# Six of w_o's eight column chunks as Strassen products, the sums of h in another order, other PSUM banks for FFN chunk 2

## The reference

```
h   = RMSNorm(x)
z   = h @ w_in                       # split among four branches a, b, c, d
y_b = branch_b(z) @ its output weight   # gated MLP, windowed attention, trailing means, conformer conv
merged = sum over the branches of sigmoid(h @ w_gate[b] + b_gate[b]) * y_b
x   = x + RMSNorm(merged @ w_o)
h2  = RMSNorm(x)
x   = x + RMSNorm((silu(h2 @ w_gate_ffn) * (h2 @ w_up_ffn)) @ w_ffn_out)
```

## Time and profile before

| | |
|---|---|
| median of 3 runs | 2610.16 us (2606.91 to 2612.08) |
| the profiled execution | 2609.34 us, of it span 2607.6 us |
| mean granted TensorE clock | 0.991 |
| PE busy | 97% |
| DVE busy | 68% |
| ACT busy | 41% |
| POOL busy | 5% |

### The profile page before, as it was taken

How to read it: one execution, slowest core, us unless ns; L and a number is a source line. 1 busy time by engine, 2 the same in 40 slices (tenths; PEclk the granted TensorE clock), 3 DMA queues, 4 the chain that set the end, 5 groups by cost and what they waited for, 6 DMA issues and landing times.

```text
span 2607.6 us, 41323 instructions
## 1 busy us (share of the span) xinstructions
PE 2536.9 (97%) x17348; PEld 1711.9 (66%) x17348; DVE 1775.5 (68%) x1962; ACT 1070.3 (41%) x1311; POOL 118.0 (5%) x96
## 2 busy tenths in 40 slices
PE   7999998999999999999979999999999999999998
PEld 3444443788788778744437888888888874444443
DVE  7985656787778777722587999999999962222223
ACT  5225432444444444433454455545455442222221
POOL 0000011000000000011320000000000000000002
PEclk9999999999999999999999999999999999999999
DMA  5231122233333233343142333333333343333331
GB/s 212 99 127 65 65 81 75 91 120 109 109 123 113 95 116 115 130 168 100 65 147 85 124 111 114 113 113 114 111 126 103 126 167 103 102 99 102 104 97 64
DMA packets 77737, 287.03 MB, mean 110 GB/s; under 512 B 8624, under 2 KB 9776, under 8 KB 76080
## 3 DMA queue, kind: packets, MB, share of 16 engines
q1 hardware_dynamic: 77616, 285.39, 32.4%
HBM read 276.97 MB, written 8.39 MB: 109 GB/s over the span
## 4 chain that ended last, share of the span: by engine, by line
PE 86%; DVE 7%; issue 3%; ACT 2%; POOL 0%; DMA 0%; DVEq 0%; SPq 0%; ACTq 0%; POOLq 0%
PE psum L1346 15%; PE psum L1347 15%; PE psum L1348 15%; PE psum L1339 13%; PE psum L1340 13%; PE psum L1341 13%; DVE wq L808 1%; ACT wq L460 1%; PE psum L1418 1%; PE psum L1443 1%; DVE region_f L1192 0%; DVE region_t L869 0%; DVE region_f L1180 0%; DVE region_f L1089 0%; DVE std L901 0%
## 5 line engine op out<-in xcount | busy, mean ns | idle before, releaser
L808 DVE SCALAR_TENSOR_TENSOR wq<-stage,wq 128x1024 f16<-128x1024 f32 (+2 forms) x668 | 801.7, 1201 | 687.3 <-ACT wq L460 681.9
L460 ACT ACTIVATE wq<-stage 128x1024 f16<-128x1024 f32 (+2 forms) x668 | 691.0, 1036 | 922.4 <-PE psum L1341 512.7
L1339 PE MATMUL psum<-region_f,wq 128*128 128x512 f16 x1616 | 615.4, 381 | 30.0 <-DVE work L1214 9.5
L1340 PE MATMUL psum<-region_f,wq 128*128 128x512 f16 x1616 | 615.1, 381 | 0.0
L1341 PE MATMUL psum<-region_f,wq 128*128 128x512 f16 x1616 | 615.0, 381 | 0.0
L1348 PE MATMUL psum<-region_t,wq 128*128 128x256 f16 x2176 | 593.6, 273 | 0.0
L1346 PE MATMUL psum<-region_t,wq 128*128 128x256 f16 x2176 | 593.5, 273 | 0.0
L1347 PE MATMUL psum<-region_t,wq 128*128 128x256 f16 x2176 | 593.5, 273 | 0.0
L1346 PE MATMUL psum<-region_f,wq 128*128 128x256 f16 x1632 | 446.3, 273 | 14.8 <-DVE region_t L869 8.9
L1347 PE MATMUL psum<-region_f,wq 128*128 128x256 f16 x1632 | 446.3, 273 | 0.0
L1348 PE MATMUL psum<-region_f,wq 128*128 128x256 f16 x1632 | 446.3, 273 | 0.0
(11 more groups left out here) (189 smaller groups left out, 1925.5 us busy)
## 6 DMA issues: line engine op xcount, KB each, us to landing
stage<-w_ffn_in_chunks SPq DMA_DIRECT2D x176, 512.0 KB, 3.9
stage<-w_gate_chunks SPq DMA_DIRECT2D x128, 512.0 KB, 4.0
stage<-w_ffn_out_chunks SPq DMA_DIRECT2D x64, 448.0 KB, 3.4
stage<-w_in_chunks SPq DMA_DIRECT2D x52, 512.0 KB, 5.3
stage<-w_o_chunks SPq DMA_DIRECT2D x32, 512.0 KB, 3.6
stage<-w_ffn_out_chunks SPq DMA_DIRECT2D x32, 512.0 KB, 3.5
stage<-w_branch_chunks SPq DMA_DIRECT2D x24, 512.0 KB, 3.5
region_f<-x_t SPq DMA_DIRECT2D x4, 1024.0 KB, 9.1
```

The source lines that it names most:

```text
L460: nc.scalar.activation(dst, stage[:, q % STAGES, 0:UNIT_W[u]], ACT.Copy, scale=WSCALE).then_inc(hi_ready, 1)
L808: V.scalar_tensor_tensor(out=slot[:, 1, 0:w], in0=stage[:, q % STAGES, 0:w], scalar=WSCALE, in1=slot[:, 0, 0:w], op0=ALU.mult, op1=ALU.sub ...
L1339: mm(to, w[:, 0, w_at:w_at + P], x_hi, start=start, stop=False)
L1340: mm(to, w[:, 0, w_at:w_at + P], x_lo, start=False, stop=False)
```

## The change

- **h's sums.** The first gates 0, 1 and 2 make three, three and two sums, gate 3 none. Windows 0 and 1 of branch c are finished at `tasks(27)` in place of `tasks(31)`.
- **w_o.** Chunks 0 and 1 stay plain, chunks 2 to 7 become Strassen products. For them merged gets its eight sums in `tset`, through a buffer `t_m` of two: sums 0 and 1 in the last gate, the others under chunks 0 and 1. TensorE waits for all eight low halves ahead of chunk 2. A tile of the output now comes out of `cb`: ACT squares it into one buffer `o_square` and copies it to `mix`. POOL signals each of its adds.
- **FFN.** Chunk 2 goes to banks 4 and 5, chunk 3 to 0 and 1 as before, so chunk 3 waits for chunk 0's eviction alone (`f_gate` 1), and the Strassen stage waits for chunk 2's (`evicted1`).
- The host puts the quarters of w_o's chunks 2 to 7 in the Strassen order. Unit numbers and semaphore targets move along.

The diff, without renumbering of targets and definitions of views:

```diff
@@ -35,6 +35,7 @@
 FFN_TURNS = 10
+FFN_BANK = (0, 2, 4, 0)
 WSCALE = 256.0
@@ -60,7 +61,7 @@
 BRANCHES = (3, 1, 0, 2)
-PLAIN_FFN = 4
+PLAIN_O, PLAIN_FFN = 2, 4
 X_SIZES = (8, 8, 7, 7, 7, 7)
@@ -240,6 +249,7 @@
         cb = view(work, 3 * HS, 2 * S, F32, "p (t s) -> p t s", t=2)
+        o_square = view(work, 3 * HS + 2 * S, S, F32)
@@ -422,11 +432,9 @@
                         pool.wait_ge(osq_ready, 2 * PAIRS * phase + 2 * p + t + 1)
-                        if t == 1:
-                            pool.wait_ge(pool_step, step.up())
-                        ins = nc.gpsimd.tensor_tensor(std[:, :], std[:, :], squares[:, t, :], ALU.add)
-                        ins.then_inc(pool_step if t == 0 else osq_used, 1)
-                    pool.wait_ge(osq_used, PAIRS * phase + p + 1)
+                        src = o_square if phase == 0 and p >= PLAIN_O else squares[:, t, :]
+                        nc.gpsimd.tensor_tensor(std[:, :], std[:, :], src, ALU.add).then_inc(osq_used, 1)
+                        pool.wait_ge(osq_used, 2 * PAIRS * phase + 2 * p + t + 1)
@@ -600,7 +608,8 @@
                 hi(u + 4)
-                t_high(2 * j)
+                if j < 3:
+                    t_high(3 * j)
                 if j == 1:
@@ -610,7 +619,10 @@
                 hi(u + 6)
-                t_high(2 * j + 1)
+                if j < 3:
+                    t_high(3 * j + 1)
+                if j < 2:
+                    t_high(3 * j + 2)
                 evict1(u + 3, sig1_0, ACT.Sigmoid, bias=vecs[:, col + 1:col + 2])
@@ -656,6 +668,11 @@
                     gate(jj, j)
+            def t_high_merged(i):
+                act.wait_ge(t_made, KP + i + 1)
+                nc.scalar.activation(tset[:, :, i, 0, :], t_m[:, i % 2, :, :], ACT.Copy).then_inc(t_hi, 1)
+
+            t_high_merged(0)
             merged_high(PAIRS - 1)
@@ -663,25 +680,65 @@
                 if t == 0 and sums > 0:
-                    act.wait_ge(osq_used, sums)
+                    act.wait_ge(osq_used, 2 * sums)
                 nc.scalar.activation(squares[:, t, :], psum[:, t, :], ACT.Square, scale=UNSCALE).then_inc(osq_ready, 1)
...
             load_sqrt_table()
-            for c in range(PAIRS):
+            t_high_merged(1)
+            t_high_merged(2)
+            for c in range(PLAIN_O):
                 u = U_O + 4 * c
                 hi(u + 4)
+                if c == 0:
+                    t_high_merged(3)
+                else:
+                    t_high_merged(7)
                 hi(u + 5)
                 norm_tile(u + 1, mix, V_POST, 2 * c, c)
+                if c == 0:
+                    t_high_merged(4)
                 hi(u + 6)
-                if c + 1 < PAIRS:
-                    hi(u + 7)
+                if c == 0:
+                    t_high_merged(5)
+                hi(u + 7)
                 norm_tile(u + 3, mix, V_POST, 2 * c + 1, c)
-            hi(U_F + 3)
+                if c == 0:
+                    t_high_merged(6)
+
+            def mixed(c, cs, t):
+
+                j = 2 * c + t
+                act.wait_ge(c_read, 4 * cs + (2 if t else 4))
+                act.wait_ge(osq_used, 2 * c + 1 - t)
+                nc.scalar.activation(o_square, cb[:, t, :], ACT.Square, scale=UNSCALE).then_inc(osq_ready, 1)
+                nc.scalar.activation(mix[:, j, :], cb[:, t, :], ACT.Copy,
+                                     scale=vecs[:, V_POST + j:V_POST + j + 1]).then_inc(evicted1 if t else evicted0, 1)
+
+            def o_chunk(c):
+                u, cs = U_OS + SU * (c - PLAIN_O), CS_O + c - PLAIN_O
+                if c == PLAIN_O:
+                    act.wait_ge(osq_used, 2 * PLAIN_O)
+                keep_product(u, cs, 0)
+                hi(u + 4)
+                hi(u + 5)
+                keep_product(u + 2, cs, 1)
+                hi(u + 6)
+                hi(u + 7)
+                keep_product(u + 4, cs, 2)
+                hi(u + 8)
+                hi(u + 9)
+                mixed(c, cs, 1)
+                hi(u + 10)
+                mixed(c, cs, 0)
+
+            for c in range(PLAIN_O, PAIRS):
+                o_chunk(c)
             act.wait_ge(m_lo, KT)
+            act.wait_ge(t_lo, 2 * KP)
             hi(U_E)
@@ -1047,8 +1104,8 @@
                     V.tensor_tensor(a_out[:, :, 1, :], a_u[:, :, :], a_out[:, :, 0, :], ALU.subtract).then_inc(a_lo, 1)
-                if k == 31:
-                    for g, w in enumerate(POOL_WINDOWS):
+                if k in (27, 31):
+                    for g, w in list(enumerate(POOL_WINDOWS))[0 if k == 27 else 2:2 if k == 27 else 4]:
                         dve.wait_ge(win_ready, g + 1)
@@ -1116,27 +1173,48 @@
                 lo(B + 4)
-                h_sums(2 * j)
-                if j == 3:
+                if j < 3:
+                    h_sums(3 * j)
+                else:
                     make_s3(U_G, 0)
                 lo(B + 5)
+                if j < 3:
+                    t_low(3 * j, t_h, 3 * j + 1)
+                    h_sums(3 * j + 1)
                 tasks(k + 1)
                 lo(B + 6)
-                t_low(2 * j, t_h, 2 * j + 1)
-                h_sums(2 * j + 1)
+                if j < 3:
+                    t_low(3 * j + 1, t_h, 3 * j + 2)
+                if j < 2:
+                    h_sums(3 * j + 2)
                 if j == 3:
...
                 lo(B + 7)
-                t_low(2 * j + 1, t_h, 2 * j + 2)
+                if j < 2:
+                    t_low(3 * j + 2, t_h, 3 * j + 3)
                 lo(B + 8)
...
+            def m_sums(i):
+
+                t = t_m[:, i % 2]
+                dve.wait_ge(m_lo, 2 * i + 2)
+                if i >= 2:
+                    dve.wait_ge(t_lo, KP + i - 1)
+                V.tensor_tensor(t.rearrange("p (h r) s -> p h r s", h=2), merged[:, :, :, i, 0, :], merged[:, :, :, i, 1, :],
+                                ALU.add).then_inc(dve_step, 1)
+                dve.wait_ge(dve_step, step.up())
+                sum_halves(t)
+
+            def m_t_low(i):
+                t_low(i, t_m[:, i % 2], KP + i + 1)
+
             def gate(jj, j):
                 u, cs = U_G + GU * (jj - 1) + (SU + 1) * j, CS_G + 4 * (jj - 1) + j
-                following = (u + SU + 1, cs + 1) if cs + 1 < CS_F else None
+                following = (u + SU + 1, cs + 1) if cs + 1 < CS_O else None
                 lo(u + 4)
@@ -1156,7 +1234,11 @@
                     make_s1(*following)
+                else:
+                    m_sums(0)
                 lo(u + 10)
+                if not following:
+                    m_sums(1)
                 lo(u + 11)
@@ -1164,10 +1246,48 @@
                     gate(jj, j)
+            m_t_low(0)
             merged_low(PAIRS - 1)
-
-            for u in range(U_O + 4, U_E + 1):
-                lo(u)
+            for i in range(2, PAIRS):
+                m_sums(i)
+                m_t_low(i - 1)
+                lo(U_O + 2 + i)
+                if i == 6:
+                    make_s3(U_OS, CS_O)
+            make_s2(U_OS, CS_O)
+            make_s1(U_OS, CS_O)
+            m_t_low(PAIRS - 1)
+            lo(U_OS + 2)
+            lo(U_OS + 3)
+
+            def o_chunk(c):
+                u, cs = U_OS + SU * (c - PLAIN_O), CS_O + c - PLAIN_O
+                following = (u + SU, cs + 1) if c + 1 < PAIRS else None
+                lo(u + 4)
+                lo(u + 5)
+                make_s4(u, cs)
+                lo(u + 6)
+                if following:
+                    make_s3(*following)
+                lo(u + 7)
+                if c > PLAIN_O:
+                    dve.wait_ge(evicted0, E_O + c)
+                    dve.wait_ge(evicted1, E_O + c)
+                c22_c21(u, cs)
+                lo(u + 8)
+                if following:
+                    make_s2(*following)
+                c11(u, cs)
+                lo(u + 9)
+                if following:
+                    make_s1(*following)
+                c12(u, cs)
+                lo(u + 10)
+
+            for c in range(PLAIN_O, PAIRS):
+                o_chunk(c)
+            lo(U_E)
+
             inverse_root(2)
@@ -1206,7 +1326,7 @@
-                bank = 2 if c == 1 else 0
+                bank = FFN_BANK[c]
                 u = U_F + 4 * c
@@ -1585,14 +1705,17 @@
-            for c in range(PAIRS):
+            for c in range(PLAIN_O):
                 u = U_O + 4 * c
...
                 plain_tile(u + 2, 1, merged, wq)
+            pe.wait_ge(t_lo, 2 * KP)
+            for c in range(PAIRS - PLAIN_O):
+                strassen(merged, U_OS + SU * c, CS_O + c)
             keep_clock(8)
-            pe.wait_ge(osq_used, PAIRS)
+            pe.wait_ge(osq_used, 2 * PAIRS)
             gathered_sums(osum_ready)
@@ -1600,12 +1723,13 @@
                 u = U_F + 4 * c
-                pe.wait_ge(f_gate, 1 if c == 2 else 3)
-                plain_tile(u, 0, h2, wq)
-                pe.wait_ge(evicted1, E_F + (1 if c == 2 else 3))
-                plain_tile(u + 2, 1, h2, wq)
-
```

(12 more changed lines are left out.)

28 lines of the change are left out of this document (18 added, 10 removed).

## The result

The changed kernel takes 2592.6 us (median of four runs, 2590.62 to 2594.63), where the kernel before took 2610.16 beside it. The ratio is 0.9937, with a 95% interval of 0.9925 to 0.9949. The change makes the kernel faster by 17.5 us by these medians and by 16.4 by the ratio (13 to 20 by its interval), where 28 were forecast. The time lies inside the range of 2573 to 2594, near its upper end. The profiled execution took 2590.65 us (its span is 2588.9), 18.7 us less than the one of before.

What follows compares the result with a forecast made beforehand. TensorE, busy 97% of the span, bounds the kernel: only dropped products, its waits and low clock give time. -14.2 + 11.7 - 14.3 + 0.3 - 11.3 = -27.8 us, from 2609.3 to 2581.5, median 2582; range 2573 to 2594.

Steps and rivals of the forecast that it cites:

- both signs: The prediction fails if TensorE waits for weight remainders in gates 1 and 2, or w_o chunks are over 18.5 us apart.
- A: w_o: the sums of merged are hidden better, the second wait and its clock fall away; 2578 us, chance 0.11.
- part 1: First gates: new order of h's sums and pool windows ends waits and half clock; 14.2 us gain, bounds 9 and 17.2.
- B: First gates don't take the third sum of h; three stages by 1 to 2 us, 2585 to 2588, chance 0.13.
- D: FFN: the wait moves to remainders of chunk 3 and the first Strassen chunk, only 3 us come; 2590, chance 0.04.
- C: w_o: the six Strassen chunks aren't bound by TensorE; 1 to 3 us a chunk, 2588 to 2600, chance 0.06.
- Part 2: Start of w_o: eight new sums of merged make TensorE wait twice; costs 11.7 us, bounds 7 and 17.
- Part 3: w_o: six Strassen chunks, each 18.33 instead of 20.72 us; 14.3 us gain, bounds 14.3 and 0.
- The end of w_o: The last square comes behind DVE's c12 and ACT's weight copy; 0.3 us more, between 0 and 2.
- Part 4: FFN: chunk 3 no longer waits for chunk 2's eviction; 11.3 us gain, bounds 11.4 and 3.
- E: w_o: the single square buffer shared by POOL and ACT sets a chunk's pace; slower, 2612 to 2625, chance 0.03.
- floor by weight loads: w_o: at 0.123 us a product Strassen would give nothing, 2596; counted within the rival of chance 0.06.

Runs made afterwards that it cites:

- e9: Kernel with the new h sums, window order and FFN banks but w_o plain: POOL's shifted adds for windows 2 and 3 cut to one column; 2582.76 us, ratio 0.9904.
- e5: The changed kernel with POOL's adds of the squares of w_o's output cut from 512 columns to 1; 2583.83 us, ratio 0.9904.
- e3: The kernel before with only w_o chunks 2 to 7 as Strassen products and the sums of merged for them; 2613.18 us, ratio 1.0023.
- e2: The kernel before with only FFN chunk 2 moved to banks 4 and 5; 2597.06 us, ratio 0.9961.

## Why the prediction came out as it did

- **Its own signs**: both signs by which the prediction said it would fail have come. TensorE waits for weight remainders in gates 1 and 2 (0.69 and 2.92 us), and the w_o chunks are 19.3 us apart, over 18.5. That the time still fell into the range is owed to the range's width. Its ends do not follow from their terms either: A with all of part 1 is 2578 - 3.0 = 2575, and B, D and half of C come to at least 2582 + 3 + 8 + 3 = 2596.
- **What bounds it**: right. All of the gain came from products not made, waits of TensorE and half clock.
- **Part 1**: the mechanism was right, its size was not: 9.2 us for 14.2. The step that failed is the hand layout of DVE and ACT, which gave every sum 2.97 us. Beside POOL's windows one took 6.4 us (371.88 to 378.26). The prediction moved the windows and counted only what DVE would no longer wait for. It did not ask which steps now ran beside them. (It has windows 0 and 1 three tasks earlier; the edit moves them by four, from 31 to 27.) The wait of 2.92 us has the half clock behind it (9 products in 3.2 us, 1.7 us lost); without the adds, in e9, the layout held to about 0.1 us. Rival B named the price (3 to 6 us) but not what would lengthen the steps. The 1.9 us before the third unit of the first Strassen gate came as laid out (1.84).
- **Part 2**: 15.9 us for 11.7. The merge is late by the 5.0 us of the forecast, and the turn of 6.3 us is right. The second wait is 5.5 us in place of 3.5: again the stretched steps, 3.1 us. The clock took more, too: the forecast put half of 1.4 us behind this wait, and 2.4 us came, and 2.9 for 2.1 behind the first one. In e5 a wait of 3.05 us still had 1.6 us behind it, and in e3 one of 6.4 us only 1.5.
- **Part 3**: 9.6 us for 14.3. The saving of 2.39 us a chunk is right, and so is the reading that DVE's busy time leaves room: 13.24 of 18.30 us at the start. But busy time was not the limit. DVE and ACT wait for each other in a chain that leaves, by the estimate above, 0.1 us of a chunk, and POOL lengthens it by 1.07. The check of ACT's order at a chunk's end, 2.3 us of 2.6, assumed that its weight copy comes on time. That is rival C, at the low end of its price (four times 1.0 us and once 0.8), by a chain that it did not name.
- **POOL**: the failing step of all three, for w_o by e5 and for the first gates by e9, where the waits go with the adds. The prediction weighed a shared port and kept the sum, because twice 1.27 us of POOL is hidden in 18.3. It looked at POOL's own time only. The add did get longer, 1.72 for 1.27 us, and that was hidden. The loss was on DVE, 1.22 to 2.29 us, at a step on which ACT and then TensorE wait. The trace of the kernel before had this price already, in the timelines of DVE and POOL at the start of the FFN: an add of L1183 takes 1.22 us at 1287.09 and 2.33 beside POOL.

```profile
1291.87 1.27 POOL L412 TENSOR_TENSOR std<-std,work 128x512 f32<-128x512 f32 x1
...
1291.89 2.33 DVE L1183 TENSOR_TENSOR region_f<-region_f 128x1024 f32<-128x1024 f32 x1
```

- **The end of w_o**: +0.3 forecast, -0.5 found, within what such gaps move between executions.
- **Part 4**: right to 0.1 us, in the whole change and alone in e2, with no wait at chunk 3 and the cover as named.
- **Rivals A, D and E** did not come. POOL's ring never held a chunk. The TensorE rate of 0.216 and 0.109 us a product held in every Strassen stage of every kernel, so no floor by weight loads appeared.

The three mis-sized terms are 5.0 + 4.2 + 4.7 = 13.9 us, less 0.8 at the end of w_o: the 13.1 us by which the parts fell short.

On the port the trace and the rule agree in kind. The Trainium skill ("SBUF — State Buffer", Who interferes with whom) says that a DVE instruction with two SBUF inputs contends with a GpSimd instruction that reads SBUF, and that the shared ports are an exclusive lock. It gives no time for this pair. The rows agree with a lock: `make_s1` ends 1.09 us after the POOL add that it began under, not at some shared rate.

## What to carry to other kernels

When work of GpSimd is moved or new work is put beside it, list the DVE steps with two SBUF operands that begin under it, add to each what is left of the GpSimd instruction, and follow who waits for them; GpSimd's own hidden time says nothing about this. Two engines with idle time can still set the pace, if each waits for the other: add up their handovers round a whole chunk, not their busy time. Weigh new feeder work (sums, copies) against how many units of the bounding engine there are to hide it: with two plain chunks the Strassen chunks of w_o cost 5 us. With three, and the sums and copies in another order, w_o takes 9 us less than all plain.
